# An even spread of weight pieces over the attention steps, weights that arrive in halves, and two products in column groups

## The reference

```python
h = x @ w_in            # gated-delta q|k|v, decay a, beta b, gate z, window q|k|v, memory q, 3 branch gates
o_g = gdn_branch(...)   # conv width 4, SiLU, l2 norm of q and k, chunked delta rule, gated RMSNorm
o_s = window attention  # 8 query heads, 2 key heads of 64, own chunk of 64 and two before, sinks
o_x = memory attention  # 4 heads of 128 into 256 memory tokens; each stream has its own memory
u = sum_b sigmoid(gate_b) * (branch_b @ w_branch[b])
x = LN1(alpha * x + u @ w_o);  x = LN2(alpha * x + relu(x @ w_up) ** 2 @ w_down)
```

## Time and profile before

| what | value |
| --- | --- |
| median of 3 runs | 1327.7 us (1325.42 to 1330.49) |
| profiled execution, its own time | 1330.73 us |
| its span, first to last instruction | 1328.9 us |
| mean granted TensorE clock | 0.968 of full |
| PE busy | 1276.5 us (96%) |
| DVE, ACT, POOL busy | 591.4, 411.4, 130.3 us |

### The profile page before, as it was taken

How to read it: one execution, slowest core, us unless ns; L and a number is a source line. 1 busy time by engine, 2 the same in 40 slices (tenths; PEclk the granted TensorE clock), 3 DMA queues, 4 the chain that set the end, 5 groups by cost and what they waited for, 6 DMA issues and landing times.

```text
span 1328.9 us, 19019 instructions
## 1 busy us (share of the span) xinstructions
PE 1276.5 (96%) x7703; PEld 1125.5 (85%) x7703; DVE 591.4 (44%) x805; ACT 411.4 (31%) x748; POOL 130.3 (10%) x88
## 2 busy tenths in 40 slices
PE   5999998999999799998999999999999999999997
PEld 5999556777776699886999998899998998899876
DVE  3564655433345844445333333544342343243247
ACT  3442421321322565655322222233331231132120
POOL 2230002102103421211000000010000000000000
PEclk9997999999988899987899999999999999999999
DMA  5224110000511712122222214101232222212231
GB/s 195 73 95 51 34 48 17 32 1 1 172 54 32 245 49 104 41 80 88 96 95 70 72 35 148 63 32 64 80 110 80 67 76 80 79 64 86 73 94 79
DMA packets 54092, 101.54 MB, mean 76 GB/s; under 512 B 12176, under 2 KB 33168, under 8 KB 53392
## 3 DMA queue, kind: packets, MB, share of 16 engines
q1 hardware_dynamic: 54032, 100.68, 23.6%
HBM read 94.20 MB, written 7.38 MB: 76 GB/s over the span
## 4 chain that ended last, share of the span: by engine, by line
PE 90%; DVE 4%; issue 3%; ACT 2%; DMA 1%; POOL 1%; SPq 0%; POOLq 0%; DVEq 0%; ACTq 0%
PE psum L573 42%; PE psum L994 21%; PE psum L641 6%; PE psum L660 6%; PE psum L620 2%; PE psum L642 2%; PE psum L932 1%; PE psum L666 1%; PE psum L604 1%; PE psum L900 1%; PE psum L828 1%; PE psum L816 1%; PE psum L1003 1%; DMA raw<-w_mix 1%; PE psum L682 1%
## 5 line engine op out<-in xcount | busy, mean ns | idle before, releaser
L573 PE MATMUL psum<-x_high,w_high 128*128 128x320 f32 x768 | 179.0, 311 | 1.4 <-DVE w_low L1368 1.4
L573 PE MATMUL psum<-x_low,w_high 128*128 128x320 f32 x768 | 178.6, 310 | 0.0
L573 PE MATMUL psum<-x_high,w_low 128*128 128x320 f32 x768 | 178.5, 310 | 0.0
L1368 DVE TENSOR_TENSOR w_low<-raw,w_high 128x1024 fp32r<-128x1024 f32 (+1 forms) x80 | 106.5, 1332 | 129.0 <-ACT w_high L1779 127.8
L1779 ACT CAST w_high<-raw 128x1024 fp32r<-128x1024 f32 (+1 forms) x80 | 90.9, 1136 | 165.8 <-PE psum L994 155.6
L573 PEld LDWEIGHTS psum<-x_high,w_high 128*128 128x128 f32 x768 | 130.1, 189 | 2.1 <-ACT arena L1929 1.6
L573 PEld LDWEIGHTS psum<-x_high,w_low 128*128 128x128 f32 x768 | 130.1, 189 | 0.0
L573 PEld LDWEIGHTS psum<-x_low,w_high 128*128 128x128 f32 x768 | 130.0, 189 | 0.0
L994 PE MATMUL psum<-w_high,hid_low 128*128 128x512 f32 x280 | 109.7, 392 | 0.0
L994 PE MATMUL psum<-w_low,hid_high 128*128 128x512 f32 x280 | 109.7, 392 | 0.0
L994 PE MATMUL psum<-w_high,hid_high 128*128 128x512 f32 x280 | 109.7, 392 | 0.0
(11 more groups left out here) (295 smaller groups left out, 2368.5 us busy)
## 6 DMA issues: line engine op xcount, KB each, us to landing
raw<-w_tiles SPq DMA_DIRECT2D x72, 512.0 KB, 3.5
raw<-w_mix SPq DMA_DIRECT2D x16, 768.0 KB, 4.3
ring<-w_h SPq DMA_DIRECT2D x14, 512.0 KB, 3.5
ring<-w_piece SPq DMA_DIRECT2D x24, 256.0 KB, 2.7
work<-w_h SPq DMA_DIRECT2D x9, 512.0 KB, 3.5
work<-cmkT SPq DMA_DIRECT2D x8, 512.0 KB, 3.7
work<-cmv SPq DMA_DIRECT2D x8, 512.0 KB, 4.9
mem_w<-w_mem SPq DMA_DIRECT2D x11, 256.0 KB, 2.6
```

Source lines behind the costliest of these rows:

```text
L573: mm = pe.matmul(ps[b0 + half][:, 0:HALF], weights[weight][:, c], act[part][:, k, half * HALF:(half + 1) * HALF], start=start and k == 0 a ...
L1368: dve.tensor_tensor(w_low[slot][:, 0:width], raw[slot][:, 0:width], w_high[slot][:, 0:width], ALU.subtract).then_inc(sem("low_out"), 1)
```

## The change

1. **Start.** PE multiplies a zeroed 128x128 block 18 times (`NWARM`) into bank 7 before any data has come. The input arrives as 1, 2, 2 and 3 feature tiles. The first two weight tiles are loaded, cast and subtracted in halves; PE takes feature tiles 0 to 3 of tile 0, then of tile 1, then 4 to 7 of tile 0, then of tile 1.
2. **Decay and beta.** The 8 weight columns, widened with zeros to 32, become the stationary side; 320 columns of `x` move, and feature tile k uses column group k % 4. DVE copies the 32-row sums out; five products with a 0/1 matrix (`group`) add the groups and turn them to tokens. They stand behind the first fill steps.
3. **Attention order.** All four `ws` units come in the first block of units, and `ms` before `mp` (between the two in the last block). Piece p goes with step p * 31 // 23: steps 3, 7, 11, 15, 19, 23, 27, 30 and 32 to 34 have none, step 31 has the last. The memory loads of the streams follow at pieces set by `cache_at`. `high_part(0)` goes to ACT's step 34, `low_part(0)` behind DVE's last step.
4. **`ms` values.** The 32 probability columns of both streams are the weights, in column group h; 128 columns of values move. A mask (`pair`) on the scale makes each row's other stream zero, so both streams add into one 128x128 result, which is copied out (`ms_rows`) and transposed in the next unit.

The diff, cut:

```diff
+NWARM = 18
+X_IN = (0, 1, 3, 5, KT)
...
         UNITS = [u for t in range(4) for u in
-                 [("wp", t, m) for m in range(4)] + [("ws", 0, p) for p in (2 * t, 2 * t + 1) if p < 4]
-                 + [("mp", t, 0), ("mp", t, 1), ("ms", 0, t)]]
+                 [("wp", t, m) for m in range(4)] + [("ws", 0, p) for p in range(0 if t else 4)]
+                 + ([("mp", t, 0), ("ms", 0, t), ("mp", t, 1)] if t == 3 else
+                    [("ms", 0, t), ("mp", t, 0), ("mp", t, 1)])]
+        PIECE_STEP = [p * (NU - 1) // (PIECES - 1) for p in range(PIECES)]
...
+            def first_weights(s, half):
+                c = slice(512 * half, 512 * half + 512)
+                load(ring[:, s * 1024:(s + 1) * 1024][:, c], w_h[s][:, c], f"wa{s}_in" if half else ("mem_in", "s0_in")[s])
...
-                        if n == (3 + e if p == 0 else min(UNITS.index(("ms", 0, p - 1)) + 4 + e, PIECES - 1)):
+                        if n == (3 + e if p == 0 else cache_at(p) + e):
...
+            pe.wait_ge(sem("dve_step"), 1)
+            for _ in range(NWARM):
+                pe.matmul(ps[7][:, 0:P], h_sb[:, 0:P], h_sb[:, 0:P], start=True, stop=True)
+            for half in range(2):
                 for s in range(2):
...
+                    for k in range(4 * half, 4 * half + 4):
...
+            pe.wait_ge(sem("widened"), 1)
+            for k in range(KT):
+                g = slice(32 * (k % 4), 32 * (k % 4) + 32)
+                for half in range(2):
+                    mm = pe.matmul(ps[4 + half][g, 0:HALF], wab_wide[:, k, :], x3[:, k, half * HALF:(half + 1) * HALF],
+                                   start=k < 4, stop=k >= 4, tile_position=(0, 32 * (k % 4)))
...
+            def ab_tokens():
+                pe.wait_ge(sem("ab_out"), 1)
+                for t in range(TT):
+                    mm = pe.matmul(ps[5][:, t * 8:t * 8 + 8], ab_rows[:, t * P:(t + 1) * P], const("group"),
+                                   start=True, stop=True)
...
+                if n and UNITS[n - 1][0] == "ms":
+                    pe.transpose(b[:, 3 * P:4 * P], ms_rows, ident)
...
-                        for h in range(H):
-                            for st in range(2):
+                        for st in range(2):
+                            for h in range(H):
                                 c = 512 * st + h * P
-                                mm = pe.matmul(b[:, h * 32 + 16 * u:h * 32 + 16 * u + 16],
-                                               cm[:, u, 1, c:c + P],
-                                               pT[:, u, st, 32 * h + 16 * u:32 * h + 16 * u + 16],
-                                               start=st == 0, stop=st == 1)
+                                r = slice(32 * h, 32 * h + 32)
+                                mm = pe.matmul(b[r, 0:P], pT[:, u, st, r], cm[:, u, 1, c:c + P],
+                                               start=u == 0 and st == 0, stop=u == 1 and st == 1,
+                                               tile_position=(0, 32 * h))
...
-                if n < PIECES:
-                    piece(n)
+                if n in PIECE_STEP:
+                    piece(PIECE_STEP.index(n))
...
+            then_wait(dve.memset(wab_wide, 0.0))
+            dve.wait_ge(sem("ab_in"), 16)
+            dve.tensor_copy(wab_wide[:, :, 0:8], wab).then_inc(sem("widened"), 1)
...
             dve.wait_ge(sem("ab_mm"), 1)
+            for half in range(2):
+                last = dve.tensor_copy(ab_rows[:, half * HALF:(half + 1) * HALF], ps[4 + half][:, 0:HALF])
+            last.then_inc(sem("ab_out"), 1)
+            dve.wait_ge(sem("ab_mm"), 2)
...
+                if UNITS[n][0] == "ms":
+                    then_wait(dve.tensor_tensor(rden[i], rden[i], pair, ALU.mult))
...
-                if n == NU:
-                    low_part(0, 0, RAWN)
...
+            low_part(0, 0, RAWN)
...
+            def first_halves(s, half):
+                c = slice(512 * half, 512 * half + 512)
+                act.wait_ge(sem(f"wa{s}_in" if half else ("mem_in", "s0_in")[s]), 16)
+                act.copy(wa[s][0][:, c], ring[:, s * 1024:(s + 1) * 1024][:, c]
+                         ).then_inc(sem("wa_high"), 1)
...
-                if n == NU - 1:
+                if n == NU + 2:
                     high_part(0, 0, 1, RAWN, first=True)
```

More of the change, by code:

```diff
@@ L48 @@
                   ("nstrict_p", P), ("nstrict_s", P), ("blk_s", P), ("bd16", P), ("off16", P), ("off32", P),
-                  ("off64", P), ("win0", 256), ("win", 256), ("snew", 240), ("tokblk", NB)):
+                  ("off64", P), ("win0", 256), ("win", 256), ("snew", 240), ("tokblk", NB),
+                  ("group", NB)):
     CONST_COLS[_name] = (_at, _n)
@@ L82, in shape_constants @@
     put("snew", np.where((x >= 112) & (x < 128), 0.0, NEG))
+    put("group", np.arange(P)[:, None] % 32 == np.arange(8)[None, :])
     put("tokblk", np.arange(P)[:, None] // ST == np.arange(NB)[None, :])
@@ L268, in build @@
         eps = sm(1)
+        wab_wide = place("wab_wide", ARENA + 12 * TOK, 32 * KT)[:, :].rearrange("p (k x) -> p k x", k=KT)
+        ab_rows = place("ab_rows", ARENA + 12 * TOK + 32 * KT, TOK)[:, :]
+        pair = sm(2)
         nm, den, es, rden = ([sm(2) for _ in range(3)] for _ in range(4))
@@ L288, in build @@
         cv_sb = work[:, 2048:3072].rearrange("p (b s) -> p b s", b=NB)
+        ms_rows = work[:, 1024:1024 + P]
         sm_sb = [a.rearrange("p (u s) -> p u s", u=2)
@@ L493, in cache_load, with cache_at @@
                 load(cm[:, e, 1, :], cmv[2 * p + e], "cm_in")
+            def cache_at(p):
+                past = UNITS.index(("ms", 0, p - 1)) + 3
+                return min([n for n in range(2, PIECES) if PIECE_STEP[n - 2] >= past] + [PIECES - 2])
             for n in range(1, PIECES):
@@ L598, in _ @@
                 h_tiles(i)
[L601 to L605, removed]
-            mm.then_inc(sem("ab_mm"), 1)
+            pe.wait_ge(sem("widened"), 1)
[4 more added lines that the diff above has]
+                                   start=k < 4, stop=k >= 4, tile_position=(0, 32 * (k % 4)))
+            mm.then_inc(sem("ab_mm"), 1)
+            def ab_tokens():
[3 more added lines that the diff above has]
+                                   start=True, stop=True)
+                mm.then_inc(sem("ab_mm"), 1)
             def memory_step(half, k):
@@ L1418, in first_gated @@
                 last.then_inc(sem("first_out"), 1)
+            then_wait(dve.tensor_reduce(pair, const("tokblk").rearrange("p (b e) -> p e b", e=2), AX.X, ALU.add))
             for n in range(NU + 1):
@@ L1425, in _ @@
                     dve.tensor_tensor(op[0][1], oG, op[0][0], ALU.subtract).then_inc(sem("op_out"), 1)
[L1426 to L1427 removed]
                 if n >= 1:
                     back(n - 1)
[L1430 to L1431 removed]
+                if n in PIECE_STEP[2::3]:
+                    first_gated(PIECE_STEP[2::3].index(n))
+            low_part(0, 0, RAWN)
             dve.wait_ge(sem("oh_out"), 2)
@@ L1809, in outputs @@
                 c = NP + 32 * m
+                if n and UNITS[n - 1][0] == "ms":
+                    last = NP + 32 * UNITS[n - 1][2]
+                    act.copy(oX[:, :, last:last + 32], b[:, 3 * P:4 * P].rearrange("p (h x) -> p h x", h=H))
                 if kind == "wp":
@@ L1818, in outputs @@
                 if kind == "ms":
-                    ins = act.copy(oX[:, :, c:c + 32], b[:, 0:P].rearrange("p (h x) -> p h x", h=H))
+                    ins = act.copy(ms_rows, b[:, 0:P])
                 ins.then_inc(sem("at_out"), 1)
@@ L1837, in _ @@
                     exponentials(n)
-                if n % 3 == 1 and n < PIECES:
-                    first_gate(n // 3)
+                if n in PIECE_STEP[1::3]:
+                    first_gate(PIECE_STEP[1::3].index(n))
                 if 2 <= n <= NU + 1:
@@ L1955, in _ @@
         def _(pool):
-            with pool.Fori(0, NPRE // 2) as i:
+            for half in range(2):
                 for s in range(2):
-                    pool.wait_ge(sem("wa_high"), 2 * i + (s + 1))
+                    c = slice(512 * half, 512 * half + 512)
+                    pool.wait_ge(sem("wa_high"), 2 * half + s + 1)
+                    pool.tensor_tensor(wa[s][1][:, c], ring[:, s * 1024:(s + 1) * 1024][:, c], wa[s][0][:, c], ALU.subtract
+                                       ).then_inc(sem("wa_low"), 1)
+            with pool.Fori(1, NPRE // 2) as i:
+                for s in range(2):
+                    pool.wait_ge(sem("wa_high"), 2 * i + (s + 3))
                     pool.tensor_tensor(wa[s][1], ring[:, s * 1024:(s + 1) * 1024], wa[s][0], ALU.subtract
```

59 lines of the change are left out of this document (29 added, 30 removed).

## The result

The changed kernel takes 1290.43 us in the median of 4 runs (1289.49 to 1291.4), the kernel before beside it 1328.77; the ratio is 0.9715, with a 95% interval of 0.9692 to 0.9737. Forecast was 1287.0 (1278 to 1300). The profiled span went from 1328.9 to 1289.2 us, by 39.7, where the sum said 40.7.

A forecast was written before the change was run, and what follows sets the result against it. PE, busy 96% of the span, was taken as the bound: its work, idle time and low clock. Gains 10.7 + 8.5 + 21.5 = 40.7 us off the 1327.7 median gave 1287.0 us, range 1278 to 1300.

The forecast's parts named there:

- Part 1: Start to end of projections: earlier first products and no gap before tile 2 gain 10.7 us, bounds 7.5 to 11.5.
- Part 2: End of projections to first norm product: new decay and beta products gain 8.5 us, bounds 3 to 10.
- Part 3: Attention up to the mix: cheaper stream memory values, spread pieces and higher clock gain 21.5 us, bounds 8 to 27.
- The second point: Start: cast and subtraction of tile 2's weights, 3.4 us, fall under tile 1's last half; tile 2 gains 1.7 us.
- feature tiles 1 to 3 arrive at a pace like that of the products: Start: these inputs keep up with PE, only 0.5 us of small waits, so the first pair ends at 21.9 us.
- The open point: Start: whether the 18 idle products raise the clock; without it the first pair loses up to 3 us.
- it was low there too: Before the first norm product: PE waits some 3 us, and the next fill steps run at low clock as before.
- two column-grouped scores among full-array work: Attention steps 3 to 23: PE lacks only 0.53 us, so tiling-mode drains would add less than 1 us.
- The step into the mix: End of attention: the mix starts 14.7 us into step 31, with PE idle about 5 us of it.
- Latency in pieceless steps: Rival, attention: pieceless steps take 3.6 us, +9, and late first mix weights add 2.5: 1298 us; chance 0.15.
- Column groups do run side by side: Rival denied this: +7 us in decay products, +2 x 4 in values, 3 of clock: 1305 us; chance 0.1.
- The granted clock in attention: Rival, slower: eight short stretches bring low clock; 100 us more at low level gives 1337 us; chance 0.02.

The follow-up runs named there:

- the last two kernels: Changed kernel plus decay products before projections, eight more idle products, POOL's output subtraction after `low_part(0)`; last piece at step 31 or 29: 1286.84 and 1284.75 us.

## Why the prediction was right, and where its terms were off

**What bounds it.** Right: PE's work, its idle places and its clock were the gain. The unedited stages moved as a block within 1.2 us, but two shifts hide in that number: the norm stage took 2.1 us more, the rest of that stretch 0.9 less. That the total came within 1.0 us of the sum, by the profiled runs, is in part luck: part 1 and the norm stage fell 5.4 us short, parts 2 and 3 and the rest gave 4.4 more.

**Part 1, 10.7, was 7.4, just below its bounds of 7.5 to 11.5.** The second point held: tile 2 follows the first pair after 0.21 us instead of 2.76, at the high level. The mis-sized step is "feature tiles 1 to 3 arrive at a pace like that of the products". The second load landed at 8.11, though its bytes and those ahead of it are fewer than had landed by 7.9 before. PE then stood for 2.06 us and ran at the low level from about 11 to 14, which an estimate from the rows puts at 1.7 us (half of 3.4). These two are the 3.1 us that the pair took more than forecast, with 0.6 gained by an earlier start (6.67 for 7.3). The open point, whether idle products raise the clock, is answered above: they do, and in three profiles of nine it was lost behind a wait of 2 us. In the best of the nine, without such a wait, tile 2 started at 22.6, where the forecast had 22.1.

**Part 2, 8.5, was 9.9.** Column groups ran side by side with four instructions to a group too: 2.33 us, against my 3.5 and 2.5 by columns. PE waited 3.24 us for ACT's squares, and the clock was low behind it, as said. But "it was low there too" is wrong as a reason to count it as nothing: before, the low clock lay in front of the first norm product, inside the stretch of 18.87 us (at 0.56), and the norm stage took 49.5 us; now it lies behind and the stage takes 51.6. The term that is missing is 2.1 us. Undone, the part cost the profiled run only 5.7 for that reason, so the gain of one stretch has to be followed into the next.

**Part 3, 21.5, was 22.6.** The sum of PE's rows for steps 3 to 30 was 131.3 + 2 and the trace has 130.89: PE was busy 130.76 of them, at 1.00, so the 2 us for latency weren't needed as waits. The pieceless steps do pay a little, 0.59 for turning instead of 0.44, 1.2 us in all, and cheaper values made that up: they took 1.01, where I took 1.5. No drain shows at L968: the turning in front of it and the scores behind it take what they take elsewhere (0.59 and 0.63 in step 11). The prediction's "two column-grouped scores among full-array work" counted too few changes of tiling, though: the window units' scores and values are tiled as well (64*128 and 128*64 in the rows), so the tiling changes in nearly every step, and PE still lacks only 0.13 of 130.89 us. The step into the mix was 15.75 instead of 14.7, and the mis-sized term is the subtraction, 2.94 and not 1.76. The transfer took 5.57 and not 4.3, which cost nothing, since it ended 11.15 us into the step, when the forecast had ACT ready at 11.3 (it was ready 0.3 us before the transfer).

**What the sum didn't say.** The total was right, but it has no parts that add: cheap values are worth 11.1 us in the changed kernel, 19.2 without the spread but with late loads, 12.1 alone; the spread is worth 2.4 us with cheap values and late loads and 10.5 with slow ones (172.4 less 161.9). And the largest single thing, 11.3 us where the pieces are at steps 0 to 23, is where the memory loads stand in SP's queue. The prediction gives that no term: the rows of before show no wait of PE for a piece's weights. That held only under slow values, and that the change moved the loads as well kept it from costing the forecast.

**The rivals.** Latency in pieceless steps is real where eleven of them follow each other (waits of 7.4 us for ACT's copies in the kernel with later loads), not where they stand alone: the changed kernel has 1.8 us of such waits, all but 0.13 of it in the last steps. Column groups do run side by side, at 2.33 and 1.01 us. The granted clock in attention went the other way: it was 0.96 and is 1.00.

## What to carry to other kernels

When a kernel's slow step gets cheap, look at which waits it had been covering: here a DMA queue that waits for that very step, with the next weights' loads behind it, took 11.3 us, as much as half of what the stretch had to gain, until the loads were placed anew. Products with 32 or fewer moving columns are candidates for a swap of sides, so that these columns become the weights in column groups, and the rows of any grouped product already in the trace price it. A wait of two or three microseconds costs more than itself where low clock follows it: look for that cost behind the wait, in the next stage. Where two parts relieve the same stretch, undo each with and without the other before giving either a number.

## What the runs showed of the hardware that I hadn't expected

- A DVE subtraction of 128x1536 took 1.76 us alone, 2.94, 3.30 and 5.14 us while POOL subtracted 128x2560; POOL's own took 5.6 to 5.75 us in all of these. DVE paid, POOL, which had started first, didn't. The rows say how much: in all five overlaps of such subtractions DVE's instruction ended as if it had stood still until POOL's end and then taken its time alone, to 0.2 us (POOL's end at 593.28, 593.90, 596.80, 597.35 and 595.15; DVE's end 1.6 us later for 128x1536, in the changed kernel, with the last piece at 29 and with the old start, and 2.7 us later for 128x2560, 2.83 alone, in the last two kernels).
- Smaller loads issued first didn't land first in proportion: with eight transfers issued within 5 us, the third in the queue (1.25 MB up to its end) landed at 8.11 us; before, with six, 1.84 MB up to the end of the third had landed at 7.9. By then about 2.2 MB had moved in both (summed from the GB/s row), so after the change more of it belonged to later transfers.
- Side by side means about four times: 16 column-grouped instructions of 256 float32 columns took 1.00 us and 4 ungrouped ones 1.06. It holds with four instructions of a group in a row: 32 of 320 columns took 2.33 us, 32 of 128 columns 1.01.
- The same code from the first norm product to the third piece took between 322.6 and 325.9 us in twelve profiles. PE's busy time in it goes from 299.5 to 303.4 us with the same instructions, which is low clock; why it lies there longer in one run than in another isn't shown, but for the 2 to 3 us behind the wait of 3.24 us.
- In the first 14 us the low clock went with the length of a wait: behind waits of 2.0 to 2.2 us the products were at half speed for some 3 us (three profiles), behind waits of up to 1.3 us they weren't (six profiles). Later, full speed outlasted a wait of 2.02 us (the last two kernels) and low clock followed one of 3.24 us (ten).
